# One encoder layer on one core: where the expert-value phase places its gathers, its residual and its last normalisation

## The reference

```python
q = (xf @ w_pq).reshape(t, PEER_HEADS, 2, PEER_HALF)
s = jnp.einsum('thpd,hpkd->thpk', q, sub_keys)
sv, si = lax.top_k(s, PEER_TOPK)
...
idx = (i1 * PEER_KEYS + i2)            # 8 heads x 16 of 16384 experts for each token
g = jax.nn.softmax(gv, axis=-1)
...
u = expert_u[idx_blk]
a = g_blk * jax.nn.gelu(jnp.einsum('tkd,td->tk', u, x_blk), approximate=False)
return jnp.einsum('tk,tkd->td', a, expert_v[idx_blk])
...
h = layer_norm(DN_ALPHA * h + ff, ln3_g[l], ln3_b[l])
```

## Time and profile before

| | |
|---|---|
| median of 3 runs | 3660.91 us (3656.52 to 3666.24) |
| profiled execution, its time | 3626.26 us |
| its span, first to last instruction | 3624.5 us |
| busy: TensorE, VectorE, GpSimd, ScalarE | 3096, 2128, 1475, 1195 us |
| products of 128 x 512 in the v phase | 3 x 1024 |
| rows gathered in the whole kernel | 1024, 512 KB each |
| bytes moved by DMA | 937 MB, mean 259 GB/s |

### The profile page before, as it was taken

One profiled execution on the slowest core, in us unless ns is written; L12 is line 12 of the kernel. 1 busy time (PEld: TensorE's weight loads), 2 busy tenths in 40 slices (PEclk: granted clock), 3 DMA queues, 4 the chain that ended last, 5 costly groups with the idle time before them and its releaser, 6 DMA issues. The chain is left out here.

```text
span 3624.5 us, 42794 instructions
## 1 busy us (share of the span) xinstructions
PE 3096.4 (85%) x16184; PEld 2401.6 (66%) x16184; DVE 2127.5 (59%) x4487; ACT 1195.0 (33%) x1931; POOL 1474.7 (41%) x1116
## 2 busy tenths in 40 slices
PE   4995989798879999999999998666468988999994
PEld 3874777677768778888777766444246656677773
DVE  4143774215432169888867776767366666655555
ACT  3212452304221143444333332887422212222221
POOL 3100002410210007555867677776545545433332
PEclk9997699899989999999999999888779999999997
DMA  4333003321322249988999999899999999999993
GB/s 157 103 100 131 1 14 127 116 87 53 134 87 71 61 167 409 347 333 326 409 410 410 409 411 406 326 396 392 394 329 360 362 354 354 365 325 323 324 324 137
DMA packets 368045, 937.45 MB, mean 259 GB/s; under 512 B 31440, under 2 KB 130264, under 8 KB 366816
## 3 DMA queue, kind: packets, MB, share of 16 engines
q0 software_dynamic: 147456, 536.94, 38.6%
q1 hardware_dynamic: 220384, 397.77, 30.9%
HBM read 827.60 MB, written 106.98 MB: 258 GB/s over the span
## 5 line engine op out<-in xcount | busy, mean ns | idle before, releaser
L1406 POOL DMA_INDIRECT ex_ring<-in_expert_v,ex_idxT_sb x406 | 468.9, 1155 | 429.1 <-PE ex_ps_v L1431 300.0
L1406 POOL DMA_INDIRECT ex_ring<-in_expert_u,ex_idx_sb x322 | 428.0, 1329 | 386.9 <-DVE ex_hg L1415 205.1
L1415 DVE CUSTOM_DVE_ANT_0 ex_ring<-ex_ring,ex_xg 128x1024 f32<-128x1024 f32 x322 | 385.0, 1220 | 118.9 <-DMA ex_ring<-in_expert_u,ex_idx_sb 117.7
L106 PE MATMUL eo_ps<-eo_v_hi_sb,aT_late_hi 128*128 128x512 f32 x1024 | 410.7, 401 | 28.1 <-DVE aT_late_lo L1979 28.1
L106 PE MATMUL ex_ps_h<-aT_late_hi,ex_uT_hi_sb 128*128 128x512 f32 x1024 | 412.6, 403 | 1.9 <-ACT ex_uT_lo_sb L1547 1.1
L107 PE MATMUL eo_ps<-eo_v_lo_sb,aT_late_hi 128*128 128x512 f32 x1024 | 402.8, 393 | 0.0
L108 PE MATMUL ex_ps_h<-aT_late_hi,ex_uT_lo_sb 128*128 128x512 f32 x1024 | 402.1, 393 | 0.0
L107 PE MATMUL ex_ps_h<-aT_late_lo,ex_uT_hi_sb 128*128 128x512 f32 x1024 | 401.2, 392 | 0.0
L108 PE MATMUL eo_ps<-eo_v_hi_sb,aT_late_lo 128*128 128x512 f32 x1024 | 401.1, 392 | 0.0
L1431 PE MATMUL ex_ps_v<-ex_ring,ex_w_sb 128*32 128x512 f32 x1624 | 266.4, 697 | 147.4 <-DMA ex_ring<-in_expert_v,ex_idxT_sb 118.7
L1986 DVE TENSOR_TENSOR eo_acc<-eo_acc,eo_ps 128x1024 f32<-128x1024 f32 x124 | 151.5, 1221 | 356.9 <-PE eo_ps L108 356.9
(11 more groups left out here) (328 smaller groups left out, 6609.7 us busy)
## 6 DMA issues: line engine op xcount, KB each, us to landing
ex_u_raw<-in_expert_u SPq DMA_DIRECT2D x128, 512.0 KB, 8.3
eo_v_raw<-in_expert_v SPq DMA_DIRECT2D x128, 512.0 KB, 6.6
act_d<-ex_act SPq DMA_DIRECT2D x128, 256.0 KB, 6.1
gate_d<-ex_gate SPq DMA_DIRECT2D x8, 4096.0 KB, 14.9
eo_g_raw<-gate_d SPq DMA_DIRECT2D x64, 512.0 KB, 6.7
eo_a_raw<-act_d SPq DMA_DIRECT2D x128, 256.0 KB, 5.4
h_d<-n_row SPq DMA_DIRECT2D x24, 512.0 KB, 2.6
pin_raw<-in_w_in SPq DMA_DIRECT2D x20, 512.0 KB, 3.9
```

Source lines behind the costliest of these rows:

```text
L106: pe.matmul(ps, l_hi, r_hi, start=first, stop=False)
L1406: pool.indirect_dma_start(rows(n), None, table, bass.IndirectOffsetOnAxis(at, 0)).then_inc(ring_in[slot[n]], 16)
L1415: dve.tensor_tensor_reduce(out=u, in0=u, in1=xg[:, j, :], scale=1.0, scalar=0.0, op0=ALU.mult, op1=ALU.add, accum_out=hg[:, j, k:k + 1]).t ...
```

## The change

1. u phase: `route` is split. A new `picked` does the reduction and, for gathered tiles, the index, before anything waits for the exponential. For tile 0 `decode`, `pick_keys` and `picked` run in one step, and dots start at step 9. TensorE's transposition of the index waits for `idx_done` alone.
2. v phase, gathers: dots end with expert 59; no call in experts 0 to 3 and 64 to 67; 32 calls in 4 to 63 and 32 in 68 to 111; none in the last 16.
3. v phase, start: the first four experts' blocks are loaded at once into the accumulator `acc`, their activations into the still empty `v_sb`. After the low parts of block t the residual of tile 4+t is loaded into `acc[t]`, and the first add is `ALPHA * acc + ps` instead of a copy.
4. v phase, end: gain and bias go to `ring`, two slots that are free after expert 111. The four gathered tiles are normalised in groups 30 and 31, between `multiply`, `low_parts` and `add`; the dense tiles follow the last adds, without the residual pass.

```diff
-            FIRST_DOT = 12
+            FIRST_DOT = 9
...
+            LAST_VALS, LN_TILES = 112, GROUPS - 2
+
+            def dots_b(e):
+                return share(DOTS_B, ETILES // 2 - 4, e) if e < ETILES // 2 - 4 else 0
+
+            def vals_b(e):
+                half = ETILES // 2
+                if GE <= e < half:
+                    return share(P // 4, half - GE, e - GE)
+                if half + GE <= e < LAST_VALS:
+                    return share(P // 4, LAST_VALS - half - GE, e - half - GE)
+                return 0
...
+                                def picked(j, n):
                                     if j >= 1:
                                         dve.wait_ge(rt_done, j)
                                     dve.wait_ge(chain, n)
                                     n = link(dve.tensor_reduce(rt[:, 1:3, :].rearrange("p q (h k) -> p h q k", h=PH),
                                                                pick[:].rearrange("p (h q) k c -> p h q k c", q=2), AX.X, ALU.add))
+                                    if j < GT:
+                                        dve.wait_ge(chain, n)
+                                        n = link(dve.scalar_tensor_tensor(idx_f[:], rt[:, 1, :], float(KEYS), rt[:, 2, :], ALU.mult, ALU.add))
+                                        dve.wait_ge(chain, n)
+                                        dve.tensor_copy(idx[:, j, :], idx_f[:]).then_inc(idx_done, 1)
+
+                                def route(j):
                                     dve.wait_ge(exp_done, j + 1)
...
                                             at[j] = decode(j)
+                                            if j == 0:
+                                                picked(j, pick_keys(j, at[j]))
...
-                    ln = RowNorm("eo_ln", sb, gain, bias, rows=(spreads[:, 0, :], spreads[:, 1, :]))
+                    ln = RowNorm("eo_ln", sb, gain, bias, rows=(ring[:, 0, :], ring[:, 1, :]))
...
                     def a_raw(e):
-                        return a_sb[:, e % 2, :]
+                        return v_sb[:, e // 2, e % 2 * DN:(e % 2 + 1) * DN] if e < GE else a_sb[:, e % 2, :]
 
                     def v_raw(e):
-                        return v_sb[:, e % 2, :]
+                        return acc[:, e, :] if e < GE else v_sb[:, e % 2, :]
...
+                            for e in range(GE):
+                                sp.dma_start(v_raw(e), v_rows[e, :, :]).then_inc(first_in[e], 16)
+                                sp.dma_start(a_raw(e), act_d[e, :, :]).then_inc(first_in[e], 16)
+                                if e % 2 == 0:
+                                    load_gates(e // 2)
...
+                                if e < 2 * GE:
+                                    t = e - GE
+                                    sp.wait_ge(v_lo_done, t + 1)
+                                    sp.dma_start(acc[:, t, :], resid[(GT + t) * P:(GT + t + 1) * P, :]).then_inc(row_in[t], 16)
+                                if e == LN_TILES * GE:
                                     sp.wait_ge(val_done, GT * P // 4)
                                     ln.load(sp)
...
                                     split(q * GE + x)
-                            for j in range(TT):
+                                    if LN_TILES <= q < LN_TILES + GT // 2:
+                                        j = 2 * (q - LN_TILES) + x // 2
+                                        if x % 2 == 0:
+                                            ln.square_root(act, j)
+                                        else:
+                                            ln.normalise(act, j, whole_row(j))
+                            for j in range(GT, TT):
...
                                 if q == 0:
-                                    dve.tensor_copy(acc[:, t, :], ps[t % 2][:]).then_inc(added[t % 2], 1)
+                                    dve.wait_ge(row_in[t], 16)
+                                    dve.scalar_tensor_tensor(acc[:, t, :], acc[:, t, :], ALPHA, ps[t % 2][:], ALU.mult, ALU.add).then_inc(added[t % 2], 1)
...
+                                    if LN_TILES <= q < LN_TILES + GT // 2:
+                                        j = 2 * (q - LN_TILES) + x // 2
+                                        if x % 2 == 0:
+                                            dve.wait_ge(sum_g, j + 1)
+                                            ln.statistics(dve, j, whole_row(j))
+                                        else:
+                                            ln.scale(dve, j)
+                                        if x % 2 == 0 and j >= 1:
+                                            ln.times_gain(dve, j - 1, whole_row(j - 1))
...
+                                if q == LAST_VALS // GE:
+                                    add_residual(dve, 3)
+                            for t in range(DT):
+                                add(GROUPS - 1, t)
+                                dve.wait_ge(added[t % 2], 2 * (GROUPS - 1) + t // 2 + 1)
+                                ln.statistics(dve, GT + t, whole_row(GT + t))
+                                ln.times_gain(dve, GT + t - 1, whole_row(GT + t - 1))
+                                ln.scale(dve, GT + t)
...
-                                    for _ in range(share(VALS_B // 4, ETILES, q * GE + t)):
+                                    for _ in range(vals_b(q * GE + t)):
                                         values(pe, done)
                                         done += 4
```

More of the change, by code:

```diff
@@ L1318, in expert_stages @@
             END_G = len(gathers)
-            for n in range(GE * (GROUPS + 1)):
-                for _ in range(share(DOTS_B, ETILES // 2, n) if n < ETILES // 2 else 0):
+            for e in range(ETILES + GE):
+                for _ in range(dots_b(e)):
                     gathers.append(("u", nu))
                     nu += 1
-                for _ in range(4 * share(VALS_B // 4, ETILES, n - GE) if n >= GE else 0):
+                for _ in range(4 * vals_b(e - GE)):
                     gathers.append(("v", nv))
@@ L1368, in expert_stages @@
             row_in = [sem(f"eo_row_in{i}") for i in range(DT)]
-            sum_done, stored = sem("eo_sum"), sem("eo_stored")
+            first_in = [sem(f"eo_first_in{i}") for i in range(GE)]
+            stored = sem("eo_stored")
             with ExitStack() as whole:
@@ L1909, in load_gates @@
                                 sp.dma_start(g_raw[:, r % 2, :, :, :], gate_d[:, :, 2 * r:2 * r + 2, :].rearrange("n p e t -> p n e t")).then_inc(g_in[r % 2], 16)
-                            load_gates(0)
-                            load_gates(1)
-                            for e in range(ETILES):
-                                if e >= 2:
+                            for e in range(GE):
[3 more added lines that the diff above has]
+                                    load_gates(e // 2)
@@ L1915, in _ @@
+                            for e in range(GE, ETILES):
+                                if e >= GE + 2:
                                     sp.wait_ge(a_lo_done, e - 1)
                                 sp.dma_start(a_raw(e), act_d[e, :, :]).then_inc(a_in[e % 2], 16)
-                                if e >= 2:
+                                if e >= GE + 2:
                                     sp.wait_ge(v_lo_done, e - 1)
+                                else:
+                                    sp.wait_ge(a_lo_done, 2 * (e - GE + 1))
@@ L1919, in _ @@
                                 sp.dma_start(v_raw(e), v_rows[e, :, :]).then_inc(v_in[e % 2], 16)
[L1920 removed]
+                                if e == GE:
+                                    load_gates(GE // 2)
+                                if e % 2 == 0 and e // 2 + 1 < ETILES // 2:
                                     load_gates(e // 2 + 1)
[L1922 to L1928 removed]
+                                if e < 2 * GE:
+                                    t = e - GE
+                                    sp.wait_ge(v_lo_done, t + 1)
+                                    sp.dma_start(acc[:, t, :], resid[(GT + t) * P:(GT + t + 1) * P, :]).then_inc(row_in[t], 16)
@@ L1990, in _ @@
                             spread_weights(dve, 2)
-                            for q in range(GROUPS + 1):
+                            for q in range(GROUPS):
                                 if q == VAL_TILE:
@@ L1994, in _ @@
                                 for x in range(GE):
-                                    if q < GROUPS:
-                                        multiply(q * GE + x)
-                                        low_parts(q * GE + x)
+                                    multiply(q * GE + x)
+                                    low_parts(q * GE + x)
                                     if q >= 1:
                                         add(q - 1, x)
-                                    if q < VAL_TILE:
```

(28 more changed lines are left out.)

37 lines of the change are left out of this document (15 added, 22 removed).

## The result

The changed kernel took 3624.73 us (median of 6 executions, 3619.48 to 3644.42), the kernel before beside it 3659.05 (6 executions, 3652.07 to 3670.12). The ratio is 0.993, interval 0.9903 to 0.9957: 25.6 us less, between 16 and 35 (the two medians alone stand 34.3 us apart). Forecast were 3639 us and 21.8 us less; the time lies in the range 3616 to 3663, and it is faster by more than 0.3%.

A forecast was written before the change was run, and what follows sets the result against it. TensorE is busiest, but DMA limits the later u phase and nearly fills in the v phase's first half; the tail idles TensorE. Terms -35.6 + 12 + 5 + 3 - 6 = -21.6, scaled to -21.8 from 3660.9: 3639 us, range 3616 to 3663.

The forecast's parts named there:

- its own sign (4): v phase: first matmul some 23 us after its start instead of 29, half reached within 3 us of today's 537 after it.
- (1) Tail: After TensorE's last instruction: 48.9 us become 13.3, a gain of 35.6.
- (2) Normalisation in groups 30 and 31: Last v-phase groups: normalising gathered tiles there makes TensorE wait for low parts, +12 us (bounds 5 and 16).
- The port step: Groups 30 and 31: GpSimd's bias blocks VectorE operations with two SBUF inputs; the term is 12 us, without it 5.
- (3) Dense calls: Experts 68 to 111: 32 calls in 44 experts instead of 22 cost +5 us (bounds 0 and 15).
- The loop's own figure: Experts 68 to 111: ring refill of 12.3 to 13.8 us against 13.0 costs 0 to 6 us in all.
- rival C: Dense stretch: rows land after 16.2 us as in the u phase, 109 us for 5, time 3743; chance 0.06.
- (4) First 64 experts: v phase's first half: earlier start, added residual bytes and denser gathers give +3 us together (-12 to +23).
- the weighing by bytes: First 64 experts: DMA share 0.97 makes bytes the nearer measure, +5.9 for the residual, -3 for the start; +3 taken.
- rival B: First half of v phase: the ring is the limit, +23 for +3, 3659 us, no change seen; chance 0.17.
- (5) Indices: u phase: indices ahead of the softmax leave 6 rows fewer after step 58, -6 us (bounds -8 and +1).

The follow-up runs named there:

- third profile: The changed kernel, unaltered, profiled on the third chip; timed there at 3619.52 us, ratio 0.994 to the kernel before.
- spread version: Changed kernel with one gathered tile normalised in each of groups 28 to 31, biases of tiles 0 to 2 and 7 on VectorE: 3600.50 us, ratio 0.9889.
- The pair with four buffers: Kernel before with four gelu-result buffers instead of two (3639.73 us, ratio 1.0002), and the same plus only the change's early indices and dots from step 9 (3629.68 us, 0.998).

## Why the prediction was right, and where its steps were off

The prediction was right in its time and in its direction. It was lucky in the sum, where four terms missed by 3 to 4 us each and cancelled, and its own sign (4) failed.

The stages of the v phase, in us, cut at the stage's first load, at VectorE's adds number 3, 59, 64, 111 and 127 (counted from 0, one for each expert) and at the span's end. All profiles with the old v phase, then all with the new one in which the stretch is unaltered:

```
                         old v phase                    new v phase
start to expert 3        55.4 54.5 56.7 56.4 56.5       52.7 51.3 52.4 51.1 53.4 52.0 52.9 52.7
expert 3 to 59           454.3 462.0 453.5 455.0 459.4  471.2 465.3 466.7 477.2 474.5 473.1 474.0 470.3
expert 59 to 64          35.1 33.6 39.0 39.7 41.9       33.6 in all
64 to 111, less ideal    none                           0.0 0.9 0.9 3.2 0.4 0.0 1.7 2.9
111 to 127, less ideal   none                           14.5 14.3 16.3 14.8
last matmul to the end   48.9                           13.3
```

(1) Tail, forecast -35.6: 48.9 became 13.3, so -35.6. Right to the row: the last tile's add, statistics, gain of the tile before, scale, normalise, gain, bias.

(2) Normalisation in groups 30 and 31, forecast +12 (bounds 5 to 16): +14.3 to +16.3. The waits were 3.9 and 6.5 for my 4.6 and 7.4; what I left to the bound, slower matmuls after the waits, is the rest: 93.24 us for 400 matmuls that take 89.41 at full clock. The port step is shown by the run without biases. Its size was 10 us for my 7 (12 less 5), 6.5 of it wait and 3.5 slower matmuls.

(3) Dense calls, forecast +5 (0 to 15): 0 to 3.2, mean 1.2. In two of eight profiles TensorE is busy for the whole of the 321.2 us; in the others it waits up to four times for gathered rows, at most 1.56 us at once (spread version). The loop's own figure was right: the refill of 12.3 to 13.8 us against 13.0 gave 0 to 6. Mis-sized was the weighing, because I went up for the share of DMA. Rows land 8.1 us after their issue there (third profile); rival C would have wanted 12.9. The rival was out by its own figure.

(4) First 64 experts, forecast +3 (-12 to +23): +6.8 as the difference of means, which is the noise of these stages too (old 544.8 to 557.8, new 550.2 to 561.9). Between the two first profiles it is 12.6 (544.8 and 557.4), where the prediction's own sign allowed 3. The sum was near, its reason was not. The start gives -3.6 for my -5; the first matmul comes 23.9 to 25.7 us after the stage's start, for 28.6 to 30.3 before and my 23. Expert 59 to 64 gives -4.3: no dots there any more, three calls as before, and no stall (33.6 = 5 x 5.44 + 3 x 2.12). In between experts 4 to 59 cost 14.7 more, 8.42 us each for 8.16; 2.1 of the 14.7 are one call more in this stretch. The step that failed is the weighing by bytes: I took them for the nearer measure because the share was 0.97, and the run with fewer gate loads gave back 1.5 to 13 us for 45 us of transfer. What is left is the ring's loop, that of rival B, but at half its price: with 3.73 entries instead of 3.5 an expert should have gone from 8.16 to 8.70 by the ring's rate, and went to 8.42.

(5) Indices, forecast -6 (-8 to +1): the first gather 27.8 us earlier, as forecast over 20, and the u phase 9.5 us shorter where it is undisturbed (994.6 and 997.7 in two profiles of the old one, mean 996.2; 984.2 to 987.4 in seven of the new one, mean 986.7). Larger than my bound of -8, which came from six rows fewer after expert 58; what gives the rest isn't shown. The pair with four buffers gives 10.7 in the profile and 8 in the times. Where the u phase is disturbed, the times can't tell this gain from the noise (1.0003), but the profiles still lean the same way: 1023.0 and 1023.4 with the old u phase, 1014.7, 1008.6 and 1019.1 with the new one.

Sum of the measured terms: -35.6 + 15.0 + 1.2 + 6.8 - 9.5 = -22.1 us, where the forecast had -21.6. Terms (2) and (4) were 3 and 4 us too small, (3) and (5) 4 us too dear; that these cancel is luck. The three ratios 0.993, 0.9962 and 0.994 are 25.6, 14 and 22 us less; the middle one is of the chip on which every profile shows a disturbed u phase. The forecast time stands 14.4 us above the measured median: 1.9 because before was taken at 3660.9 and not 3659.05, and 12.5 because the medians stand 34.3 apart and the gain was put at 21.8. By the ratio the time would be 3633.

What stays open: why TensorE's products for the gelu, or their signal, come up to 11.6 us late in the u phase of some executions and never in others of the same program. My own reading, the store of the results, is ruled out by the semaphore records. That these same profiles lack a part of their records may belong to it or not; no run shows it. And no run alters the ring, so its price in the first half rests on the chain and on what the fewer loads ruled out.

## What to carry to other kernels

When work is moved from the tail into the stream of an engine that others wait for, ask first which instruction ends the slack, and put nothing in front of it: the same four tiles cost 14.5 us inside two groups, 6.3 us behind the last low parts, and 0.8 us spread over four groups with three biases moved to VectorE. Work on an engine that nobody waits for is not free if it takes a port: three biases on GpSimd, of use to no matmul, cost 10 us, and 1.23 us each on VectorE. A DMA share near 1 does not say that bytes are the limit: take bytes away and look, before an edit is priced by them. And a wait that the profile puts down to no engine is not yet a wait for the other thing in the program: look at which signal came just before it ended, and whether the profile has all its records.

## What the runs showed of the hardware that I had not expected

Removing 15.7 MB of gate loads (512 KB each) from a stretch at share 0.96 moved a gathered row's landing from 8.4 to 7.7 us, and the stretch by 10 us where the transfer alone had been 45. A VectorE add that takes one operand from PSUM ran in 1.22 us with a GpSimd bias over it (add at 3629.35, bias 3628.24 to 3630.61 in the changed kernel's first profile), while the subtraction with two SBUF inputs took 3.37. And TensorE's signal for finished products came up to 11.6 us after the end that the profile gives for them in some executions and never over 0.04 us after it in others of the same program, with 28 us between the two u phases of before; the former profiles hold about 31000 semaphore records each, the latter over 37000.
